# Weight rows interleaved by runs of 4, 256 and 16 columns, and read by TensorE with a step

## The chip, the cores and the metric

The kernel runs on one core of a Trainium2 chip. A core has a matrix engine (TensorE, "PE" in the profile; its weight loads are listed apart as "PEld"), a vector engine (VectorE, "DVE"), a scalar engine (ScalarE, "ACT"), a general engine (GpSimd, "POOL") and a queue engine (SyncE, "SP") that here issues all DMAs. The metric is the device time of one execution in microseconds (us); less is better.

## What is computed

The reference runs two transformer blocks over 256 tokens of width 2048, in float32. The first block has two hybrid layers; the second has one, with a feed-forward part before and after it. Cut to what the change touches:

```python
def hybrid_layer(x, ...):                    # twice, layer 0 and layer 1
    proj = x @ w_in
    ...
    mix = jnp.concatenate([y_mla, y_pool, y_conv], axis=-1)
    out = mix @ w_out + b_out                # "out": the output weights
    return layernorm(DEEPNORM_ALPHA * x + out, ln_g, ln_b)

def second_block(x, mem, ...):
    x = x + 0.5 * swiglu(rms_norm(x, ffn1_norm[l]), ...)
    h = rms_norm(x, mix_norm[l])
    proj = h @ w_in[l]                       # of it, "heads": queries and keys
    fq, fk, fv, f_logit, sq, sk, sv, mq = jnp.split(proj, IN_CUTS, axis=-1)
    fq = rms_norm(fq.reshape(B, S, FOX_HEADS, HEAD_DIM), fox_q_gain[l])
    ...
    mn = rms_norm(mem, mem_norm[l])
    mk = rms_norm((mn @ w_mem_k[l])..., mem_k_gain[l])     # "mem": memory weights
    mv = (mn @ w_mem_v[l]).reshape(B, M, MEM_HEADS, HEAD_DIM)
    ...
    x = x + mixed @ w_out[l]
    x = x + 0.5 * swiglu(rms_norm(x, ffn2_norm[l]), ...)
```

## The kernel before

**Slabs.** All weights come from HBM as *slabs*: one slab is 128 partitions by up to 2048 float32 values (1 MiB). `plan()` lists the regions of the program (`in_a0`, `uq0`, ..., `out0`, `mem0`, ..., `nat0`, `heads`, `nat1`, `mixout`, `up..`, `wide..`), each with its number of slabs: 16 for each `out` region (two layers, 32 in all), 4 for each `mem` region (8 in all), 20 for `heads`. SyncE loads slab s into `raw` (4 buffers). ScalarE rounds it to a second float type into `high` (L1374), VectorE writes the remainder raw - high into `low` (L1787), each in two pieces of 1024 columns (the first piece `..._a`, the second `..._b`); `high` and `low` have two buffers each. TensorE then multiplies with both parts. So a slab passes three engines, and the semaphores `highs_a/b`, `lows_a/b`, `products` and `stored` hold the order.

**Two ways to multiply.** In regions of kind "tile" the weights are the stationary operand and the activations stream (L932 with 512 columns, L936 with 256). In regions of kind "natural" (`out`, `mem`, `heads`, `nat`) and "unit" the activations are the stationary operand (`xs`, `mixs`, `memh` or `hidden`, 128 x 128) and a run of 512 columns of the weights is the **moving operand**, streamed into a PSUM bank of 128 x 512. Each such product is three matmuls, in `product_natural` (L946, L947, L948): x_high with w_high, x_low with w_high, x_high with w_low.

**A natural slab.** It holds four blocks of weight rows (four steps of the contraction, `c` = 0 to 3) side by side, each 128 rows by 512 output columns: columns 0:512 of the slab are block 0, 512:1024 block 1, and so on (`_rows` lays them out on the host). Blocks 0 and 1 are piece 0 of the slab, blocks 2 and 3 piece 1. For each piece and each of the two groups of 128 tokens TensorE takes the blocks in turn, so a slab is 4 blocks x 2 groups x 3 = 24 matmuls of 512 columns. The slice that each one streams is contiguous:

```python
w = slice(c * 512, (c + 1) * 512)
...
last = product_natural(a, in_mix(r)[:, at_, :], high[:, pos_, w], low[:, pos_, w], b,
                       kt == 0, kt == 4 * r.per - 1)
```

The sequence of regions and what each slot of them does beside the products (attention steps, norms) is written out by hand in tables. Every SBUF tensor starts at a multiple of 32 bytes (`at` in `build`).

Of the kernel before, what the change touches and what calls it, by code (L numbers as in the profile page):

```python
# [15 lines left out]
P = 128  # L16
D = 2048
# [64 lines left out]
def plan():  # L82
# [21 lines left out]
    for r in regions:  # L104
# [9 lines left out]

        r.per = 2 if r.name[:3] == "mem" else 4
        r.kind = next((k for n, k in (("up", "unit"), ("wide", "unit"), ("down", "down"), ("uq", "uq"), ("uk", "uk"), ("uv", "uv"),
                                      ("pool", "pool"), ("mem", "natural"), ("nat", "natural"), ("heads", "natural"),
# [242 lines left out]
def build(nc, t):  # L360

    with ExitStack() as ctx:
# [566 lines left out]
        def _(eng):  # L929
# [13 lines left out]
            def product_natural(bank_, still, hi, lo, b, start, stop):  # L943
# [4 lines left out]
                return eng.matmul(bank_, xh, lo, start=False, stop=stop)  # L948

            def middle_of(r, k):  # L950

                if r.name[:4] == "in_a":
                    return 12
                if r.name[:4] == "in_b":
                    return 8 + k // 2
                if r.name[:4] == "in_d":
                    return (8, 9, 10, 11, 11 + 2 * r.layer, 12 + 2 * r.layer, 8)[k // 2]
                return 8

            def slot(r, k, i):  # L960
# [201 lines left out]
                else:  # L1162
                    group, q_ = natural_at(r, k)
                    for piece in range(2):
# [5 lines left out]
                        for b in range(TB):  # L1170
                            tile = TB * group + b
                            a = bank_free(tile, 0) if q_ == 0 and piece == 0 else bank_of(r, tile)
                            for c in range(2 * piece, 2 * piece + 2):
                                w = slice(c * 512, (c + 1) * 512)
                                kt = 4 * q_ + c
                                at_ = kt
                                if b == 0 and r.name == "nat0":

                                    wait_split(eng, "mix", kt)
                                if b == 0 and r.name[:3] == "mem":  # L1180

                                    eng.wait_ge(mem_l, 8 * r.layer + kt + 1)
                                if r.name[:3] == "out":
                                    at_ = 4 * MIX_ORDER[r.layer][q_] + c
                                    if k < 4 and b == 0 and c == 0:
                                        eng.wait_ge(mix_l, 4 * r.layer + k + 1)
                                last = product_natural(a, in_mix(r)[:, at_, :], high[:, pos_, w], low[:, pos_, w], b,
                                                       kt == 0, kt == 4 * r.per - 1)
                            if b == 0 and kt == 4 * r.per - 1:
                                last.then_inc(first_half, 1)  # L1190
# [1248 lines left out]


def _cols(v):

# [8 lines left out]
def layout(inp):  # L2451
# [21 lines left out]
    chunks = [a["w_out"][l].reshape(4, 512, D)[list(MIX_ORDER[l])].reshape(D, D) for l in range(DEPTH)]  # L2473
    out["w_out"] = np.concatenate([_rows(w, 4, 512) for w in chunks])
    rows = [(a["emb_ln_g"], a["emb_ln_b"], a["b_out"][0]), (a["ln_g"][0], a["ln_b"][0], a["b_out"][1])]
# [31 lines left out]
    out["w_first"] = np.concatenate([nat[0:3], heads[0:3], nat[3:4], heads[3:4]])  # L2507
    out["w_heads"] = heads[4:]
    out["wf"] = np.ascontiguousarray(w[:, fl].reshape(KT, P, FOX).transpose(1, 0, 2)).reshape(P, KT * FOX)
    order = list(range(FOX + SWA, FOX + SWA + MEM)) + [FOX + (2 + h) % SWA for h in range(SWA)] + list(range(FOX))  # L2510
    out["w_mixout"] = _tiles(a["w_out_2"][0].reshape(KT, P, D)[order].reshape(D, D))
    mk, mv = (_rows(a[f"w_mem_{n}_2"][0], 4, 512).reshape(DEPTH, 2, P, D) for n in "kv")
    out["w_mem"] = np.ascontiguousarray(np.stack([mv, mk], 1)).reshape(8, P, D)
    out["mem"] = np.ascontiguousarray(a["mem_2"][0].T.reshape(KT, P, S).transpose(1, 0, 2))
# [39 lines left out]
```

## Time and profile before

| | |
|---|---|
| median of 3 runs | 2531.43 us (2530.93 to 2531.8) |
| span of the profiled execution | 2529.6 us |
| PE busy | 2513.3 us (99% of the span) |
| DVE busy | 1859.2 us (73%) |
| ACT busy | 1323.1 us (52%) |
| DMA | 480.84 MB, mean 190 GB/s |

The span runs from the first to the last instruction; 1.8 us of the median lie around it. Matmuls are pipelined: a matmul is listed with the time from its issue to its modelled end, and the next one begins before that. How fast TensorE goes is therefore read from the difference of two *starts*, not from the duration in a row.

### The profile page before, as it was taken

The numbers are of one execution on the slowest core, as the hardware profiler recorded it, in microseconds if no ns is written. First come the engines' busy times: TensorE is split into PE (matmuls) and PEld (weight loads), VectorE is DVE, ScalarE is ACT, GpSimd is POOL, SyncE is SP. The second block draws the span as 40 slices with busy tenths as digits, with TensorE's granted clock in tenths as the row PEclk, the third lists the DMA queues.
The fourth block names the chain that finished last, engine by engine and source line by source line (L and its number), as shares of the span: only waits on it lengthen the run. The fifth ranks groups of instructions, "written<-read, shape, count | busy, mean of one in ns | idle before, by whom it ended". The sixth has DMA issues, their size and how long they took to land.

```text
span 2529.6 us, 33116 instructions
## 1 busy us (share of the span) xinstructions
PE 2513.3 (99%) x12088; PEld 2107.5 (83%) x12088; DVE 1859.2 (73%) x2991; ACT 1323.1 (52%) x1893; POOL 25.5 (1%) x24
## 2 busy tenths in 40 slices
PE   8999999999999999999999999999999999999999
PEld 6888888888888888888888887888888888888888
DVE  8787658787658777677777786678777767777766
ACT  6675565566566444444444455765544444444443
POOL 4000000000000000000000000000000000000000
PEclk9999999999999999999999999999999999999999
DMA  7555556455555555555555554444555555555554
GB/s 303 202 195 175 192 183 237 168 193 182 186 182 196 187 198 191 192 184 203 195 195 180 192 201 151 146 160 173 184 199 193 190 184 198 200 197 188 196 183 150
DMA packets 71231, 480.84 MB, mean 190 GB/s; under 512 B 8000, under 2 KB 10688, under 8 KB 17216
## 3 DMA queue, kind: packets, MB, share of 16 engines
q1 hardware_dynamic: 71104, 479.16, 53.4%
q8 instruction: 78, 1.28, 0.2%
q14 instruction: 49, 0.40, 0.0%
HBM read 475.72 MB, written 2.10 MB: 189 GB/s over the span
## 4 chain that ended last, share of the span: by engine, by line
PE 83%; DVE 1%; ACT 1%; issue 0%; ACTq 0%; DVEq 0%
PE acc L946 12%; PE acc L948 12%; PE acc L947 12%; PE score L946 10%; PE score L948 10%; PE score L947 10%; PE acc L932 8%; PE acc L936 4%; PE score L932 1%; PE score L1285 1%; DVE low L1787 0%; PE head_ps L1310 0%; PE score L936 0%; PE turn_ps L1294 0%; PE head_ps L1311 0%
## 5 line engine op out<-in xcount | busy, mean ns | idle before, releaser
L1787 DVE TENSOR_TENSOR low<-raw,high 128x1024 fp32r<-128x1024 f32 (+2 forms) x912 | 1079.5, 1189 | 460.2 <-ACT high L1374 451.5
L1374 ACT ACTIVATE high<-raw 128x1024 fp32r<-128x1024 f32 (+2 forms) x912 | 934.7, 1028 | 842.5 <-PE acc L948 435.9
L932 PE MATMUL acc<-xs,high 128*128 128x512 f32 x1184 | 393.4, 395 | 1.5 <-DVE xs L2331 1.2
L946 PE MATMUL acc<-high,xs 128*128 128x512 f32 x928 | 366.3, 395 | 0.3 <-DVE scale_a L1880 0.3
L948 PE MATMUL acc<-low,xs 128*128 128x512 f32 x928 | 361.6, 390 | 0.0
L947 PE MATMUL acc<-high,xs 128*128 128x512 f32 x928 | 361.1, 389 | 0.0
L936 PE MATMUL acc<-xs,low 128*128 128x256 f32 x1184 | 297.5, 278 | 0.0
L946 PE MATMUL score<-high,xs 128*128 128x512 f32 x736 | 286.4, 389 | 0.0
L948 PE MATMUL score<-low,xs 128*128 128x512 f32 x736 | 286.3, 389 | 0.0
L947 PE MATMUL score<-high,xs 128*128 128x512 f32 x736 | 286.3, 389 | 0.0
L932 PEld LDWEIGHTS acc<-xs,high 128*128 128x128 f32 x1184 | 219.2, 188 | 49.6 <-DVE xs L2331 1.9
L1834 DVE STREAM_TRANSPOSE unit_turn<-unit_prod 32x128 f32<-32x128 f32 x704 | 212.8, 302 | 9.8
L936 PEld LDWEIGHTS acc<-xs,low 128*128 128x128 f32 x1184 | 211.8, 188 | 3.9
L948 PEld LDWEIGHTS acc<-low,xs 128*128 128x128 f32 x928 | 174.2, 188 | 36.8
L946 PEld LDWEIGHTS acc<-high,xs 128*128 128x128 f32 x928 | 174.3, 188 | 36.4 <-issue 1.0
L947 PEld LDWEIGHTS acc<-high,xs 128*128 128x128 f32 x928 | 174.3, 188 | 35.5
L948 PEld LDWEIGHTS score<-low,xs 128*128 128x128 f32 x736 | 138.2, 188 | 28.7
L946 PEld LDWEIGHTS score<-high,xs 128*128 128x128 f32 x736 | 138.2, 188 | 28.7
L947 PEld LDWEIGHTS score<-high,xs 128*128 128x128 f32 x736 | 138.2, 188 | 28.6
L947 PE MATMUL score<-high,hidden 128*128 128x512 f32 x352 | 136.9, 389 | 0.0
L946 PE MATMUL score<-high,hidden 128*128 128x512 f32 x352 | 136.9, 389 | 0.0
L948 PE MATMUL score<-low,hidden 128*128 128x512 f32 x352 | 136.9, 389 | 0.0
(410 smaller groups left out, 3200.4 us busy)
## 6 DMA issues: line engine op xcount, KB each, us to landing
raw<-w_up_dram SPq DMA_DIRECT2D x176, 1024.0 KB, 4.8
raw<-w_in_dram SPq DMA_DIRECT2D x76, 1024.0 KB, 4.9
raw<-w_wide_dram SPq DMA_DIRECT2D x75, 1024.0 KB, 4.8
raw<-w_out_dram SPq DMA_DIRECT2D x32, 1024.0 KB, 4.8
raw<-w_heads_dram SPq DMA_DIRECT2D x20, 1024.0 KB, 4.8
raw<-w_mixout_dram SPq DMA_DIRECT2D x16, 1024.0 KB, 4.8
raw<-w_mem_dram SPq DMA_DIRECT2D x8, 1024.0 KB, 4.8
raw<-w_first_dram SPq DMA_DIRECT2D x8, 1024.0 KB, 4.8
```

What stands on the lines that cost most here:

```text
L932: return eng.matmul(bank_, hi, moving, start=start, stop=False)
L936: return eng.matmul(bank_[:, 0:S], lo, moving[:, 0:S], start=False, stop=stop)
L946: eng.matmul(bank_, xh, hi, start=start, stop=False)
L947: eng.matmul(bank_, xl, hi, start=False, stop=False)
L948: return eng.matmul(bank_, xh, lo, start=False, stop=stop)
L1285: last = eng.matmul(score[n % 2][:, b, 0:w], qc[:, b * P:(b + 1) * P], kc[:, 0:w], start=(m == 0), stop=(m == len(qk) - 1))
L1374: eng.activation(high[:, s % SPLIT, to:to + n * P], raw[:, s % RAW, at_:at_ + n * P], ACT.Copy).then_inc((highs_a, highs_b)[piece], 1)
L1787: eng.tensor_tensor(low[:, s % SPLIT, w], raw[:, s % RAW, at_:at_ + n * P], high[:, s % SPLIT, w].bitcast(F32), ALU.subtract).then_inc((lo ...
L1834: ins = eng.transpose(to[QUAD * j:QUAD * (j + 1), n, :, :, :], from_[QUAD * n:QUAD * (n + 1), j, :, :, :])
```

## The change

The host interleaves the two 512-column blocks of each piece. With run length r, the 1024 columns of a piece are now r columns of block 0, r columns of block 1, the next r of block 0, and so on. r is 4 for the `out` regions, 256 for `mem`, and 16 for `heads`. `nat0` and `nat1`, and all other regions, are left as they are. On the chip the moving operand of those regions becomes an access pattern of 512/r runs of r columns, with a step of 2r columns from run to run: 128 runs of 4 with a step of 8 (`out`), 32 of 16 with a step of 32 (`heads`), 2 of 256 with a step of 512 (`mem`). The k-th column that streams is the same weight column as before, and it goes to the same place of the PSUM bank. DMAs, splits, stationary operands, PSUM addresses and all semaphore waits are the same, and so is the order of the instructions on every engine: nothing is moved.

```diff
         r.per = 2 if r.name[:3] == "mem" else 4
+        r.run = {"out": 4, "mem": 256}.get(r.name[:3], 16 if r.name == "heads" else None)
...
+            def columns_in(r, slab, c):
+
+                if r.run is None:
+                    return slab[:, c * 512:(c + 1) * 512]
+                two = slab[:, c // 2 * 1024:(c // 2 + 1) * 1024]
+                return two.rearrange("p (j c i) -> p c j i", c=2, i=r.run)[:, c % 2, :, :]
+
+            def columns_out(r, bank_):
+
+                return bank_ if r.run is None else bank_.rearrange("p (j i) -> p j i", i=r.run)
...
-                                w = slice(c * 512, (c + 1) * 512)
...
-                                last = product_natural(a, in_mix(r)[:, at_, :], high[:, pos_, w], low[:, pos_, w], b,
-                                                       kt == 0, kt == 4 * r.per - 1)
+                                last = product_natural(columns_out(r, a), in_mix(r)[:, at_, :], columns_in(r, high[:, pos_, :], c),
+                                                       columns_in(r, low[:, pos_, :], c), b, kt == 0, kt == 4 * r.per - 1)
...
+def _runs(a, run):
+
+    n, p, w = a.shape
+    a = a.reshape(n, p, w // 1024, 2, 512 // run, run).transpose(0, 1, 2, 4, 3, 5)
+    return np.ascontiguousarray(a).reshape(n, p, w)
...
-    out["w_out"] = np.concatenate([_rows(w, 4, 512) for w in chunks])
+    out["w_out"] = _runs(np.concatenate([_rows(w, 4, 512) for w in chunks]), REG["out0"].run)
...
-    out["w_heads"] = heads[4:]
+    out["w_heads"] = _runs(heads[4:], REG["heads"].run)
...
-    out["w_mem"] = np.ascontiguousarray(np.stack([mv, mk], 1)).reshape(8, P, D)
+    out["w_mem"] = _runs(np.stack([mv, mk], 1).reshape(8, P, D), REG["mem0"].run)
```

## Rows read from the trace of the kernel before

**Rows 1.** Spans of the cores: span, mean granted TensorE clock
```profile
core 0: 2529.6 us, clock 1.000
```

**Rows 2.** The page's parts 1 and 2: busy us, and tenths in 40 slices
```profile
PE 2513.3 (99%) x12088; PEld 2107.5 (83%) x12088; DVE 1859.2 (73%) x2991; ACT 1323.1 (52%) x1893; POOL 25.5 (1%) x24
...
PEclk9999999999999999999999999999999999999999
```

**Rows 3.** The view of waits, whole span: us in total, times, longest us
```profile
DVE low L1787 <- ACT high L1374: 451.5, 449, 2.7
ACT high L1374 <- PE acc L948: 435.9, 283, 3.8
ACT high L1374 <- PE score L948: 344.7, 218, 2.1
```

**Rows 4.** Busy time by stretch: out0, mem0, out1, mem1, and most of heads
```profile
core 0: us, PE busy (x) PEld busy (x) DVE busy (x) ACT busy (x) POOL busy (x), PEclk, DMA share, GB/s
284.34:372.60 88.26, 87.29 (x386) 71.97 (x385) 50.55 (x54) 49.87 (x73) 0.00 (x0) 1.00 0.59 207
372.60:398.10 25.50, 25.50 (x129) 21.18 (x128) 21.58 (x38) 21.67 (x39) 0.00 (x0) 1.00 0.39 146
662.74:751.70 88.96, 87.29 (x386) 71.98 (x385) 51.16 (x56) 49.86 (x73) 0.00 (x0) 1.00 0.58 207
751.70:777.10 25.40, 25.40 (x130) 21.37 (x129) 23.27 (x45) 22.19 (x44) 0.00 (x0) 1.00 0.39 146
1545.00:1680.00 135.00, 134.14 (x650) 110.57 (x649) 93.85 (x197) 93.33 (x230) 0.00 (x0) 1.00 0.41 142
```

**Rows 5.** Timeline of TensorE in out0: start us, us, what
```profile
299.90 0.39 PE L946 MATMUL acc<-high,mixs 128*128 128x512 f32 x1
300.13 0.39 PE L947 MATMUL acc<-high,mixs 128*128 128x512 f32 x1
...
301.26 0.39 PE L946 MATMUL acc<-high,mixs 128*128 128x512 f32 x1
```

**Rows 6.** DMA issues by array: count, KB each, us to landing
```profile
raw<-w_out_dram SPq DMA_DIRECT2D x32, 1024.0 KB, 4.8
raw<-w_heads_dram SPq DMA_DIRECT2D x20, 1024.0 KB, 4.8
...
raw<-w_mem_dram SPq DMA_DIRECT2D x8, 1024.0 KB, 4.8
```

**Rows 7.** Groups in out0 (284.34 to 372.6): busy us, mean ns, idle before
```profile
L946 PE MATMUL acc<-high,mixs 128*128 128x512 f32 x128 | 49.9, 390 | 1.0 <-DVE branch L1906 1.0
L948 PE MATMUL acc<-low,mixs 128*128 128x512 f32 x128 | 49.8, 389 | 0.0
...
L1787 DVE TENSOR_TENSOR low<-raw,high 128x1024 fp32r<-128x1024 f32 x32 | 38.7, 1224 | 27.8 <-ACT high L1374 27.7
L1374 ACT ACTIVATE high<-raw 128x1024 fp32r<-128x1024 f32 x32 | 33.7, 1058 | 36.7 <-PE acc L948 36.7
```

**Rows 8.** Timeline of TensorE in the pool region, moving operands of 256 columns
```profile
202.11 0.28 PE L1149 MATMUL acc<-pooled,high 128*128 128x256 f32 x1
202.23 0.28 PE L1150 MATMUL acc<-pooled,high 128*128 128x256 f32 x1
202.35 0.28 PE L1151 MATMUL acc<-pooled,low 128*128 128x256 f32 x1
202.47 0.28 PE L1149 MATMUL acc<-pooled,high 128*128 128x256 f32 x1
```

**Rows 9.** Timeline of TensorE, plain float32 operands of 256 columns
```profile
190.00 0.59 PE L1310 MATMUL head_ps<-turned,v_mla 128*128 128x256 f32 x2
190.43 0.38 PE L1311 MATMUL head_ps<-turned,v_mla 128*128 128x128 f32 x2
```

**Rows 10.** Groups by form: contiguous operands, and operands in four runs of 256
```profile
L1374 ACT ACTIVATE high<-raw 128x1024 fp32r<-128x1024 f32 x846 | 892.1, 1057 | 770.0 <-PE acc L948 410.9 <-PE score L948 310.1 <-PE acc L936 43.2
L1725 ACT ACTIVATE mixs<-mix 128x1024 fp32r<-128x1024 f32 x12 | 12.7, 1058 | 12.2 <-DVE mix L2227 5.1 <-DVE mix L1908 3.5 <-DVE mix L2230 3.5
...
L1787 DVE TENSOR_TENSOR low<-raw,high 128x1024 fp32r<-128x1024 f32 x846 | 1032.3, 1225 | 427.8 <-ACT high L1374 420.0
...
L2218 DVE TENSOR_TENSOR mixs<-mix,mixs 128x1024 fp32r<-128x1024 f32 x12 | 14.5, 1222 | 3.7 <-ACT mixs L1725 3.6
```

## The prediction

> **What bounds the kernel now.** I read the spans first: one core, 2529.6 us, and a granted TensorE clock of 1.000 [rows 1], which is the upper of its two levels, 2.4 GHz; the row of slices shows it there all through [rows 2]. Then the busy times: PE 2513.3 us, 99% of the span, DVE 73%, ACT 52% [rows 2]. Since listed matmul times overlap, a busy PE alone proves little, so I went to the waits: ScalarE's split (L1374) waits 435.9 + 344.7 us for TensorE's last matmul of a slab half (L948), and VectorE's split (L1787) waits 451.5 us for ScalarE's [rows 3]. The splits wait for TensorE and not the other way round. The stretches that the change touches look the same: in out0 PE is busy 87.29 of 88.26 us while DVE has 50.55 and ACT 49.87, in mem0 25.50 of 25.50, in heads 134.14 of 135.00 [rows 4]. TensorE's stream is the bound there, and its unit is the step from the start of one matmul to the next.
>
> That step: in out0 one matmul starts at 299.90 and the sixth after it at 301.26 [rows 5], so 1.36 us / 6 = 226.7 ns for 512 columns. At 2.4 GHz, with one column per cycle, 512 columns are 213.3 ns. So the stream runs at one column per cycle, and 13.4 ns are left over per matmul. Reading the step, and not the 389 or 390 ns of the group rows [rows 7], matters: the group's mean can stay while the step changes, or the reverse.
>
> **The change part by part.**
>
> *What does not change.* Host layout is outside the metric. Each slab is still one DMA of 1024 KB landing after 4.8 us [rows 6]; the splits L1374 and L1787 work on contiguous halves of the slab whatever the order of the columns in it, so their 1058 and 1224 ns stay [rows 7]. Blocks 0 and 1 are interleaved inside piece 0, and 2 and 3 inside piece 1, so each matmul still needs just the piece for which it waits: no wait comes later. The output pattern, split into runs, is still contiguous and is the old address sequence. Stationary operands, and so the weight loads, are the same. All of this I cost at nothing, and it needs no cover, since no instruction is added, removed or moved.
>
> *What changes: the moving operand of three regions.* A slab gives 24 matmuls, so by the slab counts [rows 6] it is 32 x 24 = 768 matmuls in `out` (128 runs of 4), 20 x 24 = 480 in `heads` (32 runs of 16), 8 x 24 = 192 in `mem` (2 runs of 256): 1440 matmuls, 1440 x 226.7 ns = 326 us of the stream. None of this lies beside other work that would hide it: TensorE sets the end, so each ns per matmul is worth 0.77 us in `out`, 0.48 us in `heads`, 0.19 us in `mem`. And nothing is late next while TensorE grows slower, since the splits have time to spare.
>
> The trace of before has no matmul with a moving operand in runs, so I bound the cost per matmul from both sides. Upper end: the moving operand falls to the slowest column rate that full matmuls have in this trace. The plain float32 ones take 0.43 us for two of 256 columns [rows 9], so 0.84 ns per column, 430 ns for 512: +203 ns. Lower end: the 13.4 ns over the stream's 213.3 ns were a matter of reading the operand and went away: -13.4 ns. Below that nothing can fall, because one column per cycle is reached.
>
> Between these ends I take 0, from two rows. First, what are the 13.4 ns? Matmuls of the same types with 256 contiguous columns follow each other by 0.36 us / 3 = 120 ns [rows 8], which is 106.7 ns of columns and 13.3 over. Half the columns, the same excess: the excess belongs to the instruction and not to the columns, and the next 256 columns cost (226.7 - 120) / 256 = 0.417 ns each, just a cycle of 2.4 GHz. So contiguous reading shows no stall that a new pattern could deepen or take away. The weak point is that the 120 ns might be set by something else, the weight loads between them for one, and then the agreement is chance. Second, the other engines pay nothing for runs of 256: ScalarE takes 1058 ns with a destination in four runs of 256, and 1057 ns contiguous; VectorE 1222 ns with four runs, on one source and the destination, and 1225 without [rows 10]. That covers the `mem` regions best. It is far from runs of 4 at 2.4 GHz: those engines take over 1 ns per element, TensorE 0.42.
>
> *The sum.* 768 x 0 + 480 x 0 + 192 x 0 = 0. The profiled execution would again span 2529.6 us, and with the 1.8 us around it that is 2531.4, the median of before.
>
> A rule of the Trainium skill is the one that speaks against this change, since no row shows it. SBUF — State Buffer, in its section on the DMA port swizzle, says that SBUF has lines of 16 bytes, that at least two hits per line are needed, and that an access which crosses to a new line pays a penalty. Read strictly, a jump of 16 bytes over the other block's run is such a crossing. But four columns of 4 bytes from a multiple of 16 bytes are one full line, and the contiguous stream enters 128 lines per matmul just as the stepped one does; by the rule read so the sum stays 0, and with a price on each jump it would be that of the first rival. No run yet tells which reading holds.
>
> **The rivals.**
>
> *1. Each jump between runs costs a column's time (slower).* The pattern's next run would need a new address that comes a cycle late. Then the price is 0.44 ns (226.7 / 512) per jump: `out` 768 x 127 jumps x 0.44 = 43 us, `heads` 480 x 31 x 0.44 = 6.5 us, `mem` under 0.1 us. Sum +50 us, 2581. For it: nothing in the trace streams in runs. Against it: on ScalarE and VectorE three jumps in 1024 elements show no cost, though 3 cycles would hardly show [rows 10]. It decides from the first jump on, as TensorE has no slack: to be seen at all it has to be over 5 us, 0.05 ns per jump.
>
> *2. Short runs halve the rate (slower).* Runs of 4 use half of each stretch that the read fetches, and the operand comes at the rate of [rows 9]: 768 x 203 ns = +156 us, 2687; if runs of 16 suffer too, another 480 x 203 = 97 us, 2785. For it speaks only that [rows 9] show how slowly an operand can come; against it, that those rows are of another element type, so that their rate need not have to do with reading at all.
>
> *3. The 13.4 ns are a read cost by blocks (slightly slower).* 13.4 ns are 32 cycles, one for every 16 columns. If a block of 64 bytes costs a cycle to enter, then runs of 4 spread over 64 blocks instead of 32 and pay 26.8 ns, while runs of 16 fill their blocks and pay as before: 768 x 13.4 = +10.3 us, 2542. Against it are the 256-column matmuls [rows 8], which should have shown only 6.7 ns.
>
> *4. The step takes the 13.4 ns away (faster).* If contiguous reading runs twice in a row into the same busy part of memory, and a jump avoids it, `out` and `heads` win (768 + 480) x 13.4 = 16.7 us: 2515. The same 256-column rows speak against it.
>
> *5. The change does not do what it says.* The patterns could be merged into contiguous ones by the compiler. The built program holds 768, 480 and 192 matmuls with 128 x 4, 32 x 16 and 2 x 256 moving elements, so this can be left out; it would give 2531 too.
>
> **How the numbers follow.** No cost: 0.74, for the two rows above. Rival 1: 0.08, rival 2: 0.05, rival 3: 0.07, rival 4: 0.06. The predicted time is that of no cost, 2531.4. Its own range is about 2526 to 2536, for the spread of the three runs (0.9 us) and another chip or day. With rival 3 taken in the range reaches to 2543 and holds 0.81; the rest lies beyond it on both sides. 0.2%, 5.1 us, is about what a measurement of this kernel can tell from no change. Faster by more than that: 0.06 (rival 4). Slower: 0.08 + 0.05 + 0.07 = 0.20. Within: 0.74.
>
> **What would show it.** In the profile of the changed kernel, in out0, the step from a matmul's start to the next: 227 ns if I am right, 240 with rival 3, 283 with rival 1, 430 with rival 2, 213 with rival 4. The stretch of out0 from its first to its last matmul is 88.3 us now [rows 4]; it should stay, and mem0 and heads with it. Rival 1 tells itself apart by the ratio of the regions: per matmul `out` should lose four times what `heads` does. If all regions lose alike, `mem` too, then it is the form of the pattern that costs and not the jumps. ScalarE's and VectorE's splits should keep 1058 and 1224 ns. I am wrong if any stretched region shows a step off 227 ns by more than 1 or 2 ns; and if the time moves though the steps don't, the reason lies outside this argument, first of all in the clock's row [rows 2].

## The result, and the profile after

| | before | after |
|---|---|---|
| median | 2531.12 us (2530.93 to 2531.8, 5 runs) | 2540.65 us (2539.86 to 2540.86, 5 runs) |
| ratio | | 1.0037, 95% interval 1.0024 to 1.0049 |
| span of the profiled execution | 2529.6 us | 2538.3 us |

The change costs 9.5 us, 0.37%. Forecast was no change. First the clock and the busy times (spans, then part 1 and the clock's slices of the page of after):

```profile
core 0: 2538.3 us, clock 1.000
...
PE 2522.8 (99%) x12088; PEld 2107.5 (83%) x12088; DVE 1859.3 (73%) x2991; ACT 1324.6 (52%) x1893; POOL 25.5 (1%) x24
...
PEclk9999999999999999999999999999999999999999
```

The clock is the full one as before [rows 1, 2], the counts are equal to the last instruction, and only PE is busy longer: 2522.8 us in place of 2513.3, 9.5 more. PEld, DVE and ACT stay within 1.5 us. The splits still wait for TensorE, a little longer than in [rows 3]:

```profile
DVE low L1798 <- ACT high L1385: 456.9, 450, 2.7
ACT high L1385 <- PE acc L949: 442.0, 283, 4.0
```

So TensorE's stream is the bound as argued, and it became slower itself. Where, is told by the stretches. Their columns are the length, then the busy time of PE, PEld, DVE, ACT and POOL, the clock, the share of DMA and GB/s. After: out0, out1, heads, and for comparison a stretch of the feed-forward part that the change leaves alone:

```profile
283.96:374.37 90.41, 89.45 (x386) 72.08 (x385) 50.54 (x54) 50.04 (x74) 0.00 (x0) 1.00 0.58 203
664.40:755.59 91.19, 89.53 (x387) 72.15 (x386) 51.23 (x56) 50.05 (x74) 0.00 (x0) 1.00 0.57 202
1548.10:1697.80 149.70, 149.13 (x693) 118.97 (x692) 100.83 (x215) 99.70 (x239) 0.00 (x0) 1.00 0.40 139
785.00:1020.00 235.00, 235.00 (x1040) 194.62 (x1039) 172.77 (x285) 109.40 (x123) 0.00 (x0) 1.00 0.56 197
```

And heads and the feed-forward part of the kernel before, beside out0 and out1 of [rows 4] (88.26 and 88.96 us):

```profile
1544.27:1688.90 144.63, 143.77 (x694) 118.56 (x693) 100.39 (x214) 99.26 (x239) 0.00 (x0) 1.00 0.41 144
781.00:1016.00 235.00, 235.00 (x1040) 194.66 (x1039) 172.79 (x285) 109.37 (x123) 0.00 (x0) 1.00 0.56 197
```

out0 takes 2.2 us more, out1 as much, heads 5.1 us more; the feed-forward part does the same 1040 matmuls in the same 235 us. That is the loss: 4.4 + 5.1 = 9.5 us. (The spans of the two profiled executions differ by 8.7 us only. About 0.4 us of the rest is the start, where TensorE waits 6.0 us for its first input after the change and 6.4 before; the other 0.4 us is not traced.) In the timeline of TensorE in out0, after, six steps lead from 330.71 to 332.11, which is 1.40 us where [rows 5] had 1.36:

```profile
330.71 0.40 PE L948 MATMUL acc<-high,mixs 128*128 128x512 f32 x1
330.95 0.39 PE L949 MATMUL acc<-low,mixs 128*128 128x512 f32 x1
...
332.11 0.40 PE L948 MATMUL acc<-high,mixs 128*128 128x512 f32 x1
```

In heads, after, five steps from 1617.87 to 1619.06 take 1.19 us, 238 ns each:

```profile
1617.87 0.40 PE L947 MATMUL acc<-high,xs 128*128 128x512 f32 x1
1618.10 0.41 PE L948 MATMUL acc<-high,xs 128*128 128x512 f32 x1
...
1619.06 0.40 PE L949 MATMUL acc<-low,xs 128*128 128x512 f32 x1
```

A few steps are not enough, as they differ from one another by up to 18 ns. From here on **the step of a region** is the mean, over all pairs of matmuls of `product_natural` that follow each other in it, of the difference of their starts; pairs with other work between them (over 300 ns) are left out. Where all steps are over 300 ns it is the most common value, the median. Where exactly the pairs with other work end moves the mean of heads by 0.2 to 0.4 ns: it is 228.8 to 229.0 before the change, and 231.2 to 231.6 in still_cols.

| step, ns | before | after |
|---|---|---|
| out (768 matmuls) | 226.8 | 232.2 (runs of 4) |
| heads (480) | 229.0 | 240.4 (runs of 16) |
| mem (192) | 227.5 | 227.6 (runs of 256) |
| nat0 (192, not changed) | 227.0 | 227.0 |

768 x 5.4 = 4.1 us, 480 x 11.4 = 5.5 us, together 9.6 us: the steps are the whole loss. Before, heads was at 229.0 and not at 226.7 because each piece of other work disturbs the steps behind it for some ten matmuls, and in heads such work comes often. The longest run of undisturbed contiguous steps reads 227, 226, 227, 227, 226, 227 without end; with runs of 4 it becomes 231, 232, 234, 232, 236, 229, again and again; with runs of 16 the steps wander between 234 and 252. The group rows show half of it at best. For out, after:

```profile
L948 PE MATMUL acc<-high,mixs 128*128 128x512 f32 x256 | 101.4, 396 | 0.0
...
L949 PE MATMUL acc<-low,mixs 128*128 128x512 f32 x256 | 101.0, 395 | 0.0
```

They say 395 and 396 ns where [rows 7] had 389 and 390.

Two things look odd at once. The four times longer runs of heads lose twice as much as the short ones of out. And the steps don't depend on what ScalarE and VectorE do meanwhile: in out0, after, those with ScalarE busy over 90% of their length are 232.9 ns on average, those with it busy under 10% 232.0; for VectorE 232.6 and 232.3.

### The profile page after: what moved, and what is told of

Read it like the earlier page. It is cut to its first block, busy times and chain, and to the rows that moved or that the text cites. A ratio compares the mean times of both kernels' runs of the same rounds, so it can differ in the third digit from the quotient of the medians.

```text
span 2538.3 us, 33116 instructions
## 1 busy us (share of the span) xinstructions
PE 2522.8 (99%) x12088; PEld 2107.5 (83%) x12088; DVE 1859.3 (73%) x2991; ACT 1324.6 (52%) x1893; POOL 25.5 (1%) x24
## 4 chain that ended last, share of the span: by engine, by line
PE 83%; DVE 1%; ACT 0%; issue 0%; ACTq 0%; DVEq 0%
PE acc L947 12%; PE acc L948 12%; PE acc L949 12%; PE score L947 10%; PE score L949 10%; PE score L948 10%; PE acc L933 8%; PE acc L937 4%; PE score L933 1%; PE score L1296 1%; PE head_ps L1321 0%; PE score L937 0%; DVE low L1798 0%; PE turn_ps L1305 0%; PE head_ps L1322 0%; PE sums L1239 0%
## 5 line engine op out<-in xcount | busy, mean ns | idle before, releaser
L947 PE MATMUL acc<-high,xs 128*128 128x512 f32 x928 | 368.1, 397 | 0.0
L948 PE MATMUL acc<-high,xs 128*128 128x512 f32 x928 | 363.4, 392 | 0.0
L947 PE MATMUL score<-high,xs 128*128 128x512 f32 x736 | 286.4, 389 | 0.0
L948 PE MATMUL score<-high,xs 128*128 128x512 f32 x736 | 286.3, 389 | 0.0
L947 PEld LDWEIGHTS acc<-high,xs 128*128 128x128 f32 x928 | 174.3, 188 | 37.7 <-issue 0.5
L948 PEld LDWEIGHTS acc<-high,xs 128*128 128x128 f32 x928 | 174.3, 188 | 36.8
L947 PEld LDWEIGHTS score<-high,xs 128*128 128x128 f32 x736 | 138.1, 188 | 28.7
L948 PEld LDWEIGHTS score<-high,xs 128*128 128x128 f32 x736 | 138.1, 188 | 28.6
L947 PE MATMUL score<-high,hidden 128*128 128x512 f32 x352 | 136.9, 389 | 0.0
L948 PE MATMUL score<-high,hidden 128*128 128x512 f32 x352 | 136.9, 389 | 0.0
```

What stands on the lines that cost most here:

```text
L947: eng.matmul(bank_, xh, hi, start=start, stop=False)
L948: eng.matmul(bank_, xl, hi, start=False, stop=False)
```

## The experiments

All are variants of one of the two kernels, and in each the step is read region by region, so one run can hold several arms. A time without a range is that of a single execution; the granted clock was 1.000 in every profile.

### Which length costs what

swap exchanges the lengths of the regions; lens_a and lens_b have others, with the layouts of the weights to match.

```diff
-        r.run = {"out": 4, "mem": 256}.get(r.name[:3], 16 if r.name == "heads" else None)
+        r.run = {'out0': 16, 'out1': 16, 'mem0': 16, 'mem1': 16, 'heads': 4}.get(r.name)      # swap
+        r.run = {'out0': 8, 'out1': 32, 'mem0': 128, 'mem1': 128, 'heads': 64}.get(r.name)    # lens_a
+        r.run = {'out0': 1, 'out1': 2, 'mem0': 32, 'mem1': 64, 'heads': 8}.get(r.name)        # lens_b
```

> The lengths change places: runs of 16 in out0, out1, mem0 and mem1, runs of 4 in heads. Changed kernel: a matmul's step is 232.3 ns in out (runs of 4), about 240 in heads (runs of 16), 226.7 in mem (runs of 256). Theory A, the price belongs to the length of the run: out rises to about 240 ns (768 x 13.5 = 10.4 us above the kernel before), mem likewise (192 x 13.5 = 2.6 us), heads falls to about 232 (480 x 5.6 = 2.7 us): sum 2531 + 16 = 2547 us. Theory B, it belongs to the region (another stationary operand, more other work between): out and mem stay at 232 and 227, heads stays near 240: 2540 us.

Measured: 2544.54 us (2544.40 to 2544.95), ratio 1.0052 (1.0039 to 1.0066). Steps: out0 and out1 240.0, mem0 240.1, mem1 240.2, heads 232.5. Theory A: the price belongs to the length. The time is 2.5 us under the 2547 expected, in part because heads had 229.0 ns before and not 226.7, so that it costs 480 x 3.5 = 1.7 us; with out 768 x 13.2 = 10.1 and mem 192 x 12.6 = 2.4 the sum is 14.2 us for 13.2 measured.

> Correct layouts with other lengths: out0 runs of 8, out1 of 32, heads of 64, mem of 128. Theory A1, the price is one of jumps: it would fall with the length, 8 under 4. That is already in doubt, since 16 costs more than 4; then out0 shows under 230 ns per matmul. Theory A2, the moving operand and the weight load beside it read in the same memory and collide when they are in the same part of it: the price depends on how the two walks fall on one another, is largest for some middle length and fades for long ones: 8 between 232 and 240, 32 and 64 still above 227, 128 at 227.

> Correct layouts with short lengths: out0 single columns with a step of 2, out1 runs of 2 with a step of 4, heads 8, mem0 32, mem1 64. If the jumps cost, out0 with 511 of them loses at least 4 times what runs of 4 lose (5.6 ns), over 22 ns; if the reach counts (how far the operand walks, 4096 bytes in every one of these), all are alike; if a run that fills less than 16 bytes costs a second fetch, runs of 1 and 2 show a jump to well above 240 ns that runs of 4 do not have. heads with 8 should equal out0 of the run before (8 as well), if length decides.

Measured: lens_a 2537.25 us, lens_b 2704.11 us. With the runs above, the step by length of run is:

| run, columns | 1 | 2 | 4 | 8 | 16 | 32 | 64 | 128 | 256 | all 512 |
|---|---|---|---|---|---|---|---|---|---|---|
| step, ns | 452 | 451 | 232.2 | 232.8 | 240.0 | 236.7 and 237.4 | 227.7 | 227.7 | 227.6 | 226.7 |
| more than contiguous | +226 | +225 | +5.4 | +6 | +13.3 | +10 | 0 | 0 | 0 | |

(The values for 64 to 256 are those of mem, which were 227.5 before; heads with 64 shows 228.9, before 229.0. heads with 8 equals out0 with 8: 232.8 in both.) In out0 of lens_b TensorE's timeline reads, with single columns:

```profile
320.12 0.63 PE L947 MATMUL acc<-high,mixs 128*128 128x512 f32 x1
320.57 0.63 PE L948 MATMUL acc<-high,mixs 128*128 128x512 f32 x1
321.02 0.63 PE L949 MATMUL acc<-low,mixs 128*128 128x512 f32 x1
```

Three regimes then. Runs of 1 and 2 halve the rate. Runs of 4 to 32 cost 5 to 13 ns, and not in order of their jumps: 127 jumps cost 5.4 ns, 31 cost 13.3. Runs of 64 and more, 256 bytes, are free. "If the jumps cost" is out: 511 jumps cost as much as 255. Of theory A2 of lens_a the values for 8, 32 and 128 came, and the one for 64 did not: it shows no loss, where some was expected.

### The first regime: 16 bytes

Runs of 1 and of 2 touch every stretch of 16 bytes in 4096 bytes, 256 of them; a contiguous operand and runs of 4 or more touch 128. If a stretch takes 4 cycles of 2.4 GHz, 256 are 427 ns. (This is an estimate from the 451 ns, less the 13 to 27 ns that every matmul here has over the time of its columns.) shift8 puts `high` and `low` 8 bytes off, so that a run of 4 lies over two stretches:

```diff
-        high = at("high", [P, SPLIT, 16 * P], F32R)
+        high = at("high", [P, SPLIT * 16 * P + 8], F32R)
+        high = high[:, 2:2 + SPLIT * 16 * P].rearrange("p (s w) -> p s w", s=SPLIT)
```

(and `low` the same). The longer tensors also move `low` by 32 bytes and everything behind it, the stationary operands among them, by 64.

> The changed kernel with `high` and `low` beginning 8 bytes (2 columns) past a multiple of 32 bytes; the layouts are right for it. Theory L: the moving operand comes in stretches of 16 bytes, each of which takes 4 cycles of 2.4 GHz, so a matmul takes the larger of a cycle per column and 4 cycles per stretch touched. That is from single columns and runs of 2: 256 stretches x 4 = 1024 cycles = 427 ns, and 451 measured. With the shift a run of 4 lies over two stretches: out 256 stretches, about 451 ns instead of 232; heads (runs of 16, 5 stretches instead of 4) 160 stretches, 640 cycles = 267 ns plus 13 to 27, so 280 to 294 instead of 240; mem 130 stretches, 217 + 13 = 230; contiguous operands 129, 2 ns more at most. Sum about 2540 + 168 + 22 + up to 9000 x 1.7 ns = 15: 2730 to 2745 us. Theory J, runs of 1 and 2 are slow because of the number of jumps (255 and more), not because of what a stretch holds: nothing changes, 2540 us.

Measured: 2776.93 us; out 453 ns, heads 284.5, mem 236.1, contiguous operands 233.3. In heads:

```profile
1800.18 0.46 PE L949 MATMUL acc<-high,xs 128*128 128x512 f32 x1
1800.48 0.45 PE L950 MATMUL acc<-high,xs 128*128 128x512 f32 x1
1800.76 0.45 PE L951 MATMUL acc<-low,xs 128*128 128x512 f32 x1
```

Theory L holds where it had something to say: 451 and 280 to 294 were expected. It missed the contiguous operands, 6.6 ns slower in place of 2 at most, which makes most of the 32 us by which the whole run lies above its range, and mem, 236.1 ns for 230. As the stationary operands moved by 64 bytes too, this run can't tell what of it is the offset of 8 bytes. It was the first sign that the place of the operands matters. The Trainium skill, SBUF — State Buffer, in its section on the DMA port swizzle, has the lines of 16 bytes and asks for at least two hits per line to hide the access; here runs of 2 have two hits per line and take 451 ns. The measurement decides: at one column of 4 bytes per cycle all four must be used.

A second look at this comes with the run gaps, which has other jumps between runs (and streams other columns than those of the block, so its output means nothing):

```diff
+        r.run = {'out0': 16, 'out1': 16, 'heads': 4, 'mem0': 32, 'mem1': 8}.get(r.name)
+        r.gap = {'out0': 24, 'out1': 20, 'heads': 6, 'mem0': 48, 'mem1': 12}.get(r.name)
...
+                return two[:, 0:512 // r.run * r.gap].rearrange("p (j i) -> p j i", i=r.gap)[:, :, 0:r.run]
```

> Other jumps between the runs. It streams other columns than those of the block and so computes something else. out0: runs of 16 with a step of 24 (jump over 8 columns), out1: runs of 16 with a step of 20 (over 4), heads: runs of 4 with a step of 6 (each second run crosses a multiple of 16 bytes), mem0: runs of 32 with a step of 48, mem1: runs of 8 with a step of 12. If the price of 16 (13.4 ns) is one of 128 bytes from run to run, steps of 96 and 80 bytes show less than 240. If any break in a long run costs, they stay at 240. By theory L heads has 64 runs in one stretch and 64 over two, 192 stretches x 4 = 768 cycles = 320 ns plus 13 to 27: 333 to 347 ns.

Measured: 2591.31 us; heads 340 ns, within the 333 to 347 of theory L (192 stretches):

```profile
1650.36 0.52 PE L949 MATMUL acc<-high,xs 128*128 128x512 f32 x1
1650.70 0.52 PE L950 MATMUL acc<-low,xs 128*128 128x512 f32 x1
1651.04 0.52 PE L948 MATMUL acc<-high,xs 128*128 128x512 f32 x1
```

out0 (16 of 24) 233.3, out1 (16 of 20) 240.0, mem0 (32 of 48) 232.0, mem1 (8 of 12) 233.4. All have 128 full stretches, so the second regime is something else, and a simple rule for the jump fails: one of 4 columns costs the full 13 ns, one of 8 columns half of it.

### The second regime: is it the weight load?

The 13.4 ns over the columns' own time were called fixed in the prediction. still_cols leaves the contiguous operands of before and changes what is loaded beside them; its output is another one.

```diff
-                xh, xl = still[:, b * P:(b + 1) * P], still[:, S + b * P:S + (b + 1) * P]
+                at_b = b * P if step == 1 else b
+                xh, xl = (still[:, e + at_b:e + at_b + (cols - 1) * step + 1:step] for e in (0, S))
+                bank_ = bank_[0:cols, :]
...
+                                                       cols={"out0": 64, "heads": 32}.get(r.name, P),
+                                                       step=2 if r.name == "out1" else 1)
```

> Built from the kernel before, with contiguous moving operands everywhere; the stationary operand changes. It computes something else: out0 loads 64 columns instead of 128 and writes 64 rows of the output, heads loads 32, out1 loads 128 columns with a step of 2 (every second token). Theory A, the 13.4 ns above 512 columns at 2.4 GHz are a fixed cost of the instruction or of the moving operand: all three stay at 226.7 ns. Theory B, each four columns (16 bytes) that the weight load reads take one cycle from the moving operand, 32 cycles in all for 128 columns: out0 with 64 columns shows 213.3 + 6.7 = 220 ns, heads with 32 shows 217, and out1, whose load walks over twice the bytes, 213.3 + 26.7 = 240 ns.

Measured: 2535.82 us; out0 (64 columns loaded) 230.1, heads (32) 231.6 (229.0 with the whole load), out1 (every second token) 233.3. Both theories fall. A half or a quarter of the load makes the stream slower, not faster, so the load does not take its time from the stream cycle by cycle; but the excess isn't fixed either. The same with the moving operand in runs of 16 (out0 with 32 columns loaded, out1 with every second token) and of 4 (heads, 32 columns), as above with these lengths:

> Runs of 16 in out0 with a stationary operand of only 32 columns (it computes 32 rows of the output), runs of 16 in out1 with a stationary operand of every second token, runs of 4 in heads with 32 stationary columns. Theory W, what runs of 16 and 4 lose is a collision with the weight load beside the stream: with a quarter of the load, out0 falls from 240 to about 231 ns, the step that contiguous operands show with 32 stationary columns, and heads to 231; out1 changes too, since the load walks another way. Theory M, it belongs to the moving operand alone: out0 and out1 stay near 240, heads near 232.

Measured: 2541.83 us; out0 240.3, out1 237.8, heads 231.0 (232.5 with the whole load). A quarter of the load leaves 240 as it is, so the main arm of theory W falls. Its other two came about as it said, heads at 231.0 and a change in out1, but they lie within 1 to 2 ns of what theory M expected. Last, one column read 128 times as the stationary operand, again with an output of its own:

```diff
+        r.run = {'out1': 16, 'heads': 16, 'mem0': 4}.get(r.name)
+        r.same = {'out0': 0, 'out1': 0, 'heads': 16, 'mem0': 0, 'mem1': 0}.get(r.name)
...
+                if same is not None:
+                    xh, xl = (still[:, e + same:e + same + 1].to_broadcast([P, P]) for e in (0, S))
```

> It computes something else: the stationary operand is one column read 128 times (step 0), so the weight load stays at one place of the 256-byte period: at its beginning in out0, out1, mem0 and mem1, 64 bytes further in heads. Moving operands: contiguous in out0 and mem1, runs of 16 in out1 and heads (even blocks walk the first and third 64 bytes of each 256, odd blocks the second and fourth), runs of 4 in mem0. Theory C, weight load and stream collide where they are in the same part of the period: with runs of 16 the even blocks cost more than the odd ones in out1 and less in heads, and the cheaper ones come near 216 ns. Theory S, the stream alone makes the excess: out1 and heads stay at 240 for both kinds of block, out0 at 226.7.

Measured: 2543.26 us; out0 231.7, out1 239.5, heads 241.0, mem0 230.8, mem1 231.5. In out1 the even blocks take 237.1 ns on average and the odd ones 241.9, nearly all of it in one of six steps (250 ns, from the start of the first matmul of an odd block to the next). Theory C wanted the even ones dearer there, and the reverse in heads; heads shows 239.5 and 242.1, the same way round. So theory C falls; theory S gave 240 right and 226.7 wrong.

### The second regime: the place of the operands

shift64 puts 64 bytes between `low` and all tensors behind it, the stationary operands among them:

```diff
         low = at("low", [P, SPLIT, 16 * P], F32R)
+        cursor[0] += 64
```

> All tensors behind `low` (the stationary operands xs, mixs and memh among them) lie 64 bytes further; runs of 16 in out0 and heads, of 4 in out1, mem contiguous. If stationary and moving operands collide by their addresses (theory W), the steps of 240 (out0, heads) and 232 (out1) move by several ns, and perhaps the contiguous 226.7 too. Theory M: 240, 232 and 226.7 as before the shift.

Measured: 2589.89 us. The contiguous matmuls of `product_natural` go from 226.7 to 233.3 ns in the whole program; out0 (16) 237.8, heads (16) 239.2, out1 (4) 232.2. Theory M falls on the contiguous ones. Theory W's several ns show there and hardly in the interleaved ones, which move by 0 to -2.2 ns. So the price of the place and the price of the length do not add: at this distance runs of 4 are 1.1 ns faster than contiguous operands. The same 110 us window in the feed-forward part, first in shift64:

```profile
1020.00:1130.00 110.00, 110.00 (x473) 88.65 (x472) 73.78 (x105) 46.70 (x52) 0.00 (x0) 1.00 0.52 183
```

and in the kernel before:

```profile
1020.00:1130.00 110.00, 110.00 (x487) 91.11 (x486) 77.61 (x112) 46.36 (x51) 0.00 (x0) 1.00 0.54 191
```

473 matmuls in place of 487, at the same clock, with no instruction of this stretch changed but for its addresses. Four runs with all operands contiguous ask what place it is: all64 shifts every tensor (64 bytes ahead of `raw`), the others give each stationary operand a distance of its own, such as in place_a:

```diff
+        cursor[0] += 32
         xs = at("xs", [P, KT, 2 * S], F32R)
...
+        cursor[0] += 128
         work = cursor[0]
...
-        mixs = at("mixs", [P, KT, 2 * S], F32R, work)
+        mixs = at("mixs", [P, KT, 2 * S], F32R, work - 64)
...
+        cursor[0] += 96
         memh_at = cursor[0]
```

> The kernel before with every SBUF tensor, `raw`, `high` and `low` among them, 64 bytes further; the places of stationary and moving operands to one another are those of before. With 64 bytes between `low` and the stationary operands (run shift64) contiguous matmuls took 233.4 ns in place of 226.7. Theory R, it is the place of one operand relative to the other: 226.7 ns and 2531 us again. Theory P, the place in memory of the stationary operand: 233.4 ns, about 2588 us.

> The kernel before, contiguous operands, with the stationary operands at other distances from `high` and `low`: xs (up, nat, heads) +32 bytes, mixs (out) +96, hidden (wide) +160, memh (mem) +256. Theory R: the step is a function of that distance modulo some power of two, 226.7 at 0 and 233.4 at 64; some distance may give less than 226.7. If the period is 256 bytes, memh shows 226.7. Theory F, the 13.4 ns are fixed and shift64 was another effect of moving tensors: all of them show 226.7 or all 233.4.

> As place_a with xs +192 bytes, mixs +224, hidden +320, memh +384. If the period is 128 bytes, xs (192) and hidden (320) show the 233.4 ns of 64 bytes, memh (384) shows 226.7, and mixs (224) what mixs at 96 showed; if it is 256 bytes, only hidden (320) shows 233.4.

> As place_a with xs +128 bytes, mixs +256, hidden +352, memh +512. memh at 512 shows 226.7 in any theory R, since the stationary slices lie 512 bytes apart and showed one step for all of them; xs at 128 shows 226.7 if the period is 128 bytes; mixs at 256 as memh at 256 in place_a.

Measured: all64 2531.69 us and 226.7 ns; place_a 2582.45, place_b 2576.65, place_c 2579.56 us. The window of before, in all64, with the 487 matmuls back:

```profile
1020.00:1130.00 110.00, 110.00 (x487) 91.09 (x486) 77.60 (x112) 46.34 (x51) 0.00 (x0) 1.00 0.55 190
```

Theory R holds: it is the distance of the stationary operand from `high` and `low`, in bytes modulo 256. A period of 128 is out, since 128 shows 232.9 ns and 384 shows 232.2. The mean over each stationary tensor:

| distance modulo 256 | 0 | 32 | 64 | 96 | 128 | 160 | 192 | 224 |
|---|---|---|---|---|---|---|---|---|
| step, ns | 226.7 (mixs, +256: 226.8) | 233.3 | 233.3 to 233.5 (+320: 233.3) | 234.3 (+352: 234.3) | 232.9 (+384: 232.2) | 233.3 | 231.0 | 233.3 |

memh at +256 and +512 shows 228.0 and 227.8, 227.5 before. No distance is faster than 0 for these matmuls. (The expectation of place_b had 233.4 ns at 320 alone; 224 shows it too.)

That is not so for all matmuls of the kernel. In the pool region the roles are exchanged: the weights are stationary and 256 columns of `pooled` stream. They took 120 ns in [rows 8], and in shift64 they take 0.34 us / 3 = 113 ns, all 20 of them 113 or 114:

```profile
203.34 0.28 PE L1162 MATMUL acc<-pooled,high 128*128 128x256 f32 x1
203.46 0.28 PE L1163 MATMUL acc<-pooled,high 128*128 128x256 f32 x1
203.57 0.28 PE L1164 MATMUL acc<-pooled,low 128*128 128x256 f32 x1
203.68 0.28 PE L1162 MATMUL acc<-pooled,high 128*128 128x256 f32 x1
```

Here 64 bytes make the step shorter by 6 ns, where they made that of `product_natural` longer by 6.6. The best distance is therefore a matter of the kind of matmul. The regions of kind "tile" point the same way: a matmul of 512 columns and the one of 256 behind it take 347.6 ns together before, 347.4 in place_a, 352.3 in place_b and 351.2 in place_c. In place_a they lose nothing, at the 32 bytes that cost `product_natural` 6.6 ns.

For `product_natural`, 256 bytes, 64 columns, is also the length of run from which the interleaving is free. runs_64 puts that to the test as a version of the change:

```diff
-        r.run = {"out": 4, "mem": 256}.get(r.name[:3], 16 if r.name == "heads" else None)
+        r.run = {'out': 64, 'mem': 64}.get(r.name[:3], 64 if r.name == 'heads' else None)
```

> The changed kernel with runs of 64 columns in all three kinds of region: 256 bytes, the period that the places of the operands have shown, so within 256 bytes the moving operand looks contiguous. Theory R: 226.7 ns, the time of before, 2531.3 us (between 2530.5 and 2532.5). If any interleaving costs, over 2533.

Measured: 2531.26 us (2530.84 to 2531.55), ratio 1.0000 (0.9991 to 1.0009); out 226.8, heads 228.9, mem 227.5. Interleaving in whole pieces of 256 bytes costs nothing.

low64 at last moves only `low` (64 bytes further, and all behind it another 192, so that `high` and the stationary operands keep a distance of 0):

> The kernel before, contiguous, with only `low` 64 bytes further; the stationary operands lie 256 bytes further, so that their distance to `high` is 0 modulo 256 as before. Of three matmuls of a product, two stream from `high` (L946, L947) and one from `low` (L948); after L948 the next one streams from `high` again. Theory D, each stream is disturbed by the stationary operand that is loaded beside it: L946 and L947 keep 226.7 ns, L948 rises to about 233. Theory H, the handing over from one stream to the next counts, by the place where one ends and the other begins: the steps at the two changes between `high` and `low` change and the step from L946 to L947 keeps 226.7.

Measured: 2570.08 us, 232.0 ns. Neither theory: the steps that begin with L946's, L947's and L948's counterparts are 232.6, 231.3 and 232.2 ns on average. They repeat with a period of fifteen (241, 224, 226, 229, 232, 233, 231, 236, 230, 230, 233, 235, 232, 231, 237), of which these rows show a part:

```profile
320.20 0.39 PE L949 MATMUL acc<-high,mixs 128*128 128x512 f32 x1
320.43 0.39 PE L950 MATMUL acc<-low,mixs 128*128 128x512 f32 x1
320.65 0.39 PE L948 MATMUL acc<-high,mixs 128*128 128x512 f32 x1
320.88 0.40 PE L949 MATMUL acc<-high,mixs 128*128 128x512 f32 x1
```

Moving one of the three operands changed the steps of all three matmuls, and the order of long and short steps comes back only after fifteen. So a step is not set by its own two operands alone. That the steady 226.7 is a rhythm in which each matmul leaves the next in the same position is a reading of this, not shown.

### Do the parts add up?

out_only keeps the interleaving of out alone (runs of 4), heads_only that of heads alone (16).

> Only the out regions interleaved (runs of 4), heads and mem contiguous as before. If the loss is the sum of the steps, this part is 768 x (232.2 - 226.8) = 4.2 us: 2535.4 us. If something else than the steps had been at work between the regions, it would be off this by over 1 us.

> Only heads interleaved (runs of 16). 480 x (240.4 - 229.0) = 5.5 us: 2536.7 us; the two parts together should give the 9.5 us of the changed kernel.

Measured: out_only 2535.44 us (2535.03 to 2536.08), ratio 1.0017 (1.0008 to 1.0026); heads_only 2536.11 us (2535.77 to 2537.07), 1.0019 (1.0010 to 1.0028), with 2531.28 for before beside them. 4.2 + 4.8 = 9.0 us, against 9.5 for both. In out_only, out0 shows 232.2 ns and out1 233.3, with the same runs of 4 in the same places as in the changed kernel, where both show 232.2: the step for one layout can settle 1 ns apart. In heads_only the stretch of heads is as long as in the changed kernel:

```profile
1544.30:1694.20 149.90, 149.34 (x694) 119.09 (x693) 101.03 (x216) 99.86 (x239) 0.00 (x0) 1.00 0.40 140
```

## Why the prediction was wrong, point by point

**The bound.** Right. TensorE's stream sets the end, and each ns of step came out in the time one for one: 9.6 us of steps, 9.5 us of time. It was also right to leave the group's mean and go by the steps.

**What does not change.** Right. DMAs, splits, order and waits are as they were; DVE and ACT are busy for the same time.

**The cost of the moving operand in runs: the step that failed.** The prediction took 0 between -13.4 and +203 ns, "from two rows". The first row was the one of 256 columns: 120 ns, hence an excess of 13.3 with half the columns, hence "the excess belongs to the instruction". It does not: on the same instructions with the same 512 contiguous columns it is 13.4, 17.7 or 21.0 ns by the distance of two operands alone. And the very row on which it rests changes with the addresses: in shift64 the 256 columns take 113.3 ns, an excess of 6.7 and not 13.3. The weak point named beside it, that the agreement might be chance, was the one that mattered: at distance 0 the two excesses happen to be nearly equal. One row that agrees to 0.1 ns is no proof when nothing in it varies what the change varies, here the addresses. What the runs showed in place of 0 is +5.4 ns for each of the 768 matmuls of `out` and +11.4 for each of the 480 of `heads`. The second row, four runs of 256 on the slower engines, was right for what it covered: `mem` lost nothing. It was carried over to runs of 4 and 16, which it doesn't cover.

A sign stood in the trace of before and wasn't used: contiguous steps were not all 226.7. Behind other work they ran 229, 233, 236, 224, 231, 236, 228, 233, 231, 226, and only then settled. A fixed cost does not do that. Something with a position in time or in memory was at work, and it could cost up to 9 ns in a step.

**The rivals.** The time lies within 1.4 us of rival 3's, and the mechanism is still not that one: rival 3 put 10.3 us into `out` and nothing into `heads`, since runs of 16 fill their blocks of 64 bytes; measured is 4.1 and 5.5 us. It was right in one thing, that the 13.4 ns can grow with the pattern. What the prediction held against it and against rival 4, the 256-column rows, is void, since they show half the excess in shift64. The nearness in time is chance. Rival 1 (jumps) falls by the order of the lengths: out should have lost four times what heads loses per matmul, and loses half. Rival 2, half the rate, is real, but its threshold lies below the change: it starts at runs of 2, where 16-byte stretches are half used, not at 4. It had the right size, +225 ns measured for +203. Rival 4 didn't come; the matmuls of 512 columns went under 226.7 on average in no region. Rival 5 is out by the steps.

**The rule that was weighed.** By the reading of full lines, a step of one line costs nothing. That holds for the rate, 128 lines either way, and says nothing of the 5 to 13 ns. The Trainium skill, TensorE: Matmul & The Clock Gate, in Part 2, What happens when you issue a matmul, says besides that the moving operand and the weight load have independent read ports, so that a load doesn't take from the stream. The trace agrees in that a quarter of the load gives nothing back (240.3 for 240.0 ns), but not in full: the distance of the two operands moves the step by up to 7.6 ns (234.3 for 226.7).

**What stays open.** Shown is that the loss is the longer step of out and heads, that it goes by the length of the run and is gone from 64 columns on, and that the step of contiguous operands goes by their distance modulo 256 bytes. That both have one cause is likely by the common 256 bytes, and not shown. Nor did a run split the output pattern in the PSUM bank and leave the moving operand whole. The output alone can't be it, as 32 runs of 16 cost 6.5 ns with a step of 24 columns and 13.3 with one of 20 or 32; but a part of it is not ruled out. What happens inside the 256 bytes, why 16 is the dearest length and why a jump of 4 columns costs more than one of 8, is not settled: theories C, W, D and H each failed on a number. No run kept stationary and moving operands in different halves of the 256 bytes.

## What to carry to other kernels

In a kernel that TensorE's stream bounds, a moving operand's layout in SBUF is part of its cost. Its float32 runs should be whole 16-byte stretches, since runs of 1 and 2 columns double the time, and at least 256 bytes long, or each matmul here loses 5 to 13 ns of 227. The distance between stationary and moving tensors is worth a test: for activations stationary and 512 columns streaming, multiples of 256 bytes were the best of eight, and distances of 32, 96 and 160 bytes cost this kernel 51 us (place_a). For other kinds of matmul another distance can be better, as in the pool region. Before an excess over the ideal is called fixed, look whether it is the same in all its instances, and at a row in which what the change varies was varied.

## What the runs showed of the hardware

- Matmuls of 128 x 128 by 512 columns of the second float type come every 226.7 ns at 2.4 GHz when both operands are contiguous and lie at distance 0 modulo 256 bytes (the three matmuls of `product_natural`), and every 231.0 to 234.3 ns at seven other distances (233.3 at 32, 64, 160 and 224; 234.3 at 96).
- The same at distance 0 with a moving operand in runs: 452 and 451 ns for runs of 1 and 2 columns, 232.2 for 4, 232.8 for 8, 240.0 for 16, 236.7 and 237.4 for 32, and no loss from 64 on. By a cost of 4 cycles of 2.4 GHz per 16 bytes touched, runs of 4 that start 8 bytes off (453 ns), runs of 16 that do (284.5 ns) and runs of 4 with a step of 6 (340 ns) are right within 13 to 27 ns, the excess that all of them have.
- With 256 columns streaming over stationary weights the step is 120 ns before and 113.3 in shift64, whose only difference there is 64 bytes between the two.
- Loading fewer stationary columns does not shorten the step: 231.6 ns with 32, 230.1 with 64, 229.0 and 226.8 with 128 in the same regions.
- Steps are coupled: they fall into repeating patterns, of 3 matmuls (before), 6 (runs of 4), 7 (mixs in place_a), 15 (low64) or 24 (runs of 16 in swap), and after other work on TensorE it takes some ten of them to settle.
